# A two-block transformer on one core: two expert pairs written out ahead of TensorE's loop, transposed rows copied out one PSUM bank at a time, and the last gathers held back

## The reference, cut to what matters

```
g_w        = softmax(h @ grp_w + b)[g_sel]
e_p, e_i   = top_k(softmax(expert logits of that group), 2)
weight     = g_w * e_p / sum(e_p)
hid        = silu(xb @ w_gate[e]) * (xb @ w_up[e])
out[tok]  += (hid @ w_down[e]) * weight
```

## Time and profile before

| | us |
|---|---|
| median of 3 runs | 2176.9 (2175.75 to 2178.42) |
| the profiled execution | 2185.39 |
| its span in the trace | 2183.7 |
| PE busy | 1885.3 (86% of the span) |
| DVE busy | 1046.7 (48%) |
| ACT busy | 558.5 (26%) |

### The profile page before, as it was taken

One profiled execution on the slowest core, in us unless ns is written; L12 is line 12 of the kernel. 1 busy time (PEld: TensorE's weight loads), 2 busy tenths in 40 slices (PEclk: granted clock), 3 DMA queues, 4 the chain that ended last, 5 costly groups with the idle time before them and its releaser, 6 DMA issues.

```text
span 2183.7 us, 38376 instructions
## 1 busy us (share of the span) xinstructions
PE 1885.3 (86%) x15590; PEld 1368.7 (63%) x15590; DVE 1046.7 (48%) x1922; ACT 558.5 (26%) x1189; POOL 18.8 (1%) x30
## 2 busy tenths in 40 slices
PE   7999987787766789897677777799999999999998
PEld 4744654443433457664344444399988989998997
DVE  5678541010100135542111111377888787788876
ACT  4436631111111123531111110214430021443001
POOL 0100000000000010000000000000000000000000
PEclk9999999999989999998888888999999999999999
DMA  8489249999899994369999999852345545234552
GB/s 360 159 351 426 109 197 402 422 418 429 321 429 429 425 359 179 148 250 423 429 429 428 429 429 429 368 231 105 129 174 193 193 181 235 94 139 174 193 193 97
DMA packets 52501, 628.21 MB, mean 288 GB/s; under 512 B 7088, under 2 KB 8112, under 8 KB 14256
## 3 DMA queue, kind: packets, MB, share of 16 engines
q1 hardware_dynamic: 45008, 611.30, 68.3%
q0 software_dynamic: 2592, 8.91, 1.1%
q10 hardware_dynamic: 4800, 6.56, 0.8%
HBM read 614.43 MB, written 12.32 MB: 287 GB/s over the span
## 4 chain that ended last, share of the span: by engine, by line
PE 52%; DMA 33%; DVE 10%; issue 2%; ACT 1%; SPq 1%; POOL 0%; ACTq 0%; POOLq 0%; DVEq 0%
DMA ring<-in_ex_down 17%; DMA ring<-in_ex_up 14%; PE ps L1435 7%; PE ps L1437 7%; PE ps L1436 6%; PE ps L1917 5%; PE ps L2079 4%; PE ps L2081 4%; PE ps L2080 4%; PE ps L1924 3%; PE ps L1789 1%; DVE w_lo L2987 1%; DMA ring<-in_w_static 1%; PE ps L1817 1%; DVE cat L2507 1%
## 5 line engine op out<-in xcount | busy, mean ns | idle before, releaser
L1917 PE MATMUL ps<-ring,E 128*32 128x256 f32 x5312 | 364.2, 435 | 180.1 <-DMA ring<-in_ex_gate 113.3
L1917 PEld LDWEIGHTS ps<-ring,E 128*32 128x32 f32 x5312 | 214.2, 125 | 337.1 <-issue 270.2
L1437 PE MATMUL ps<-hn_hi,w_lo 128*128 128x256 f32 x928 | 262.3, 283 | 0.0
L1924 PE MATMUL ps<-ring,E 128*32 128x512 f32 x1344 | 163.7, 629 | 31.6 <-DMA ring<-in_ex_down 30.9
L2884 DVE TENSOR_TENSOR E<-E,ps 128x256 f32<-128x256 f32 x25 | 10.5, 422 | 369.0 <-PE ps L1917 369.0
L1437 PEld LDWEIGHTS ps<-hn_hi,w_lo 128*128 128x128 f32 x928 | 177.6, 191 | 0.0
L1435 PE MATMUL ps<-hn_hi,w_lo 128*128 128x256 f32 x480 | 138.2, 288 | 1.7 <-DVE w_lo L2987 1.7
L1436 PE MATMUL ps<-hn_lo,w_lo 128*128 128x256 f32 x480 | 135.6, 283 | 0.0
L2987 DVE TENSOR_TENSOR w_lo<-ring,w_hi 128x4096 fp32r<-128x4096 f32 x30 | 132.8, 4425 | 1.0
L1435 PE MATMUL ps<-hn_hi,w_hi 128*128 128x256 f32 x448 | 126.9, 283 | 0.0
L1436 PE MATMUL ps<-hn_lo,w_hi 128*128 128x256 f32 x448 | 126.8, 283 | 0.0
(11 more groups left out here) (568 smaller groups left out, 3491.2 us busy)
## 6 DMA issues: line engine op xcount, KB each, us to landing
ring<-in_ex_up SPq DMA_DIRECT2D x64, 2048.0 KB, 18.7
ring<-in_ex_gate SPq DMA_DIRECT2D x62, 2048.0 KB, 17.3
ring<-in_ex_down SPq DMA_DIRECT2D x61, 2048.0 KB, 19.2
ring<-in_w_layer SPq DMA_DIRECT2D x56, 2048.0 KB, 8.2
ring<-in_w_static SPq DMA_DIRECT2D x32, 2048.0 KB, 15.3
y_rows<-E ACTq DMA_DIRECT2D x100, 64.0 KB, 7.8
ring<-in_ex_down SPq DMA_DIRECT2D x6, 1024.0 KB, 19.7
y_rows<-pcp POOLq DMA_DIRECT2D x18, 256.0 KB, 10.2
```

Source lines behind the costliest of these rows:

```text
L1437: return pe.matmul(out, lo, xhi, start=False, stop=last)
L1917: ins = pe.matmul(ps[lane(u, h), 2 + w, 0:HALF], xg[:, k, lane(u, h) if j is None else quad(j, u)], weights[u][:, h * HALF:(h + 1) * HALF] ...
L1924: ins = pe.matmul(ps[lane(u, c), bank, :], hid[:, m % 2, lane(u, m // 2)], slab(4 + u, (EC, D))[:, m, half_cols(c)], start=m == 0, stop=m ...
```

## The change

- **A.** The first two pairs of the first mixture stand written out ahead of PE's loop. The plan's wait and PE's two register loads move behind them; the loop runs from 1.
- **B.** `turned_out` copies each bank of transposed rows by itself as soon as its four transposes are done (`xg_mm` counts banks), and `products` waits for the second bank only at k = 4. This holds for both mixtures.
- **C.** In the first mixture the ranks' transpose goes to bank 5 and stands between the two halves of the first `turn`.
- **D.** The first `build` of one-hot matrices no longer steps the slot numbers (`iota2`); that add stands after the `token_low` calls behind it.
- **E.** At the end of the first mixture ACT weights tile 3 behind the root; POOL waits for tile 1's second choice before it issues the four gathers of tiles 2 and 3; SP loads the first w_in slab when tile 1's first choice has landed.

```diff
-            sp.wait_ge(yg_in[1][1], 16)
+            sp.wait_ge(yg_in[1][0], 16)
             static_loads(stream_b)
...
+                act.wait_ge(ssq_mm, ssq_at(call) + KC)
+                act.activation(stdv[...], ps[:, bank, 0:NX], ACT.Sqrt, bias=eps, scale=1.0 / D).then_inc(std_ready, 1)
                 if g == 0:
                     weigh(NTM - 1)
-                act.wait_ge(ssq_mm, ssq_at(call) + KC)
-                act.activation(stdv[...], ps[:, bank, 0:NX], ACT.Sqrt, bias=eps, scale=1.0 / D).then_inc(std_ready, 1)
...
                 def turned_out(count):
-                    act.wait_ge(sems["xg_mm"], count)
-                    at = turn_bank(l)
-                    act.activation(xg, ps[:, at:at + 2, :]..., ACT.Copy).then_inc(sems["xg_ready"], 1)
+                    for c in range(2):
+                        act.wait_ge(sems["xg_mm"], 2 * count - 1 + c)
+                        act.activation(xg[:, 4 * c:4 * c + 4, :], ps[:, turn_bank(l) + c, :]..., ACT.Copy).then_inc(sems["xg_ready"], 1)
...
                 gather(1, True)
                 if l == 0:
+                    turn(1, (0,))
                     pe.wait_ge(m_ready, 2)
-                    pe.matmul(ps[0:1, 2, 0:MAXB], rsc[:, 7, 0:1], ident[:, 0:MAXB], start=True, stop=True).then_inc(pos_mm, 1)
+                    pe.matmul(ps[0:1, 5, 0:MAXB], rsc[:, 7, 0:1], ident[:, 0:MAXB], start=True, stop=True).then_inc(pos_mm, 1)
+                    turn(1, (1,))
+                    pe.sem_inc(sems["gu_mm"], 2)
...
-                    pe.wait_ge(plan_ready, 1)
-                    pairs = pe.value_load(...)
-                    final = pe.value_load(...)
-                    pe.sem_inc(sems["gu_mm"], 2)
...
                         for k in range(KC):
+                            if j == 0 and w == 0 and k % 4 == 0:
+                                pe.wait_ge(sems["xg_ready"], 2 * s + 3 + k // 4)
...
-                with pe.Fori(0, final) as s:
+                for j in range(2):
+                    pair(0, j, False)
+                pe.wait_ge(plan_ready, 1)
+                pairs = pe.value_load(...)
+                final = pe.value_load(...)
+                with pe.Fori(1, final) as s:
                     pair(s, 0, False)
                     pair(s, 1, False)
...
-                    dve.tensor_tensor(iota2, iota2, lane_step, ALU.add)
+                    if not first:
+                        dve.tensor_tensor(iota2, iota2, lane_step, ALU.add)
...
             for n in range(NTM):
+                if n == QT:
+                    pool.wait_ge(yg_in[1][1], 16)
                 for k in range(2):
                     pool.indirect_dma_start(out=yg[n][k], ...).then_inc(yg_in[n][k], 16)
```

More of the change, by code:

```diff
@@ L916, in group_stats @@
                     act.activation(sqb[:, k % 4, 0:NX], xT[:, g, k, :], ACT.Square).then_inc(sq_ready, 1)
+                act.wait_ge(ssq_mm, ssq_at(call) + KC)
+                act.activation(stdv[:, g * NX:g * NX + NX], ps[:, bank, 0:NX], ACT.Sqrt, bias=eps, scale=1.0 / D).then_inc(std_ready, 1)
                 if g == 0:
                     weigh(NTM - 1)
-                act.wait_ge(ssq_mm, ssq_at(call) + KC)
-                act.activation(stdv[:, g * NX:g * NX + NX], ps[:, bank, 0:NX], ACT.Sqrt, bias=eps, scale=1.0 / D).then_inc(std_ready, 1)
             def group_modulate(call, g):
@@ L1147, in turned_out @@
                 def turned_out(count):
-                    act.wait_ge(sems["xg_mm"], count)
-                    at = turn_bank(l)
-                    act.activation(xg, ps[:, at:at + 2, :].rearrange("p b (k s) -> p (b k) s", s=PAIR), ACT.Copy).then_inc(sems["xg_ready"], 1)
+                    for c in range(2):
+                        act.wait_ge(sems["xg_mm"], 2 * count - 1 + c)
+                        act.activation(xg[:, 4 * c:4 * c + 4, :], ps[:, turn_bank(l) + c, :].rearrange("p (k s) -> p k s", s=PAIR), ACT.Copy).then_inc(
+                            sems["xg_ready"], 1)
                 def gathered(count, first=False):
@@ L1155, in gathered @@
                     turned_out(count)
+                act.sem_inc(sems["xg_ready"], 2)
                 gathered(1, True)
@@ L1903, in experts @@
                     keep_x(0)
-                turn(1)
-                if l == 1:
+                    turn(1)
                     pe.wait_ge(mod_ready, 2 + 1)
                     keep_x(1).then_inc(sems["gu_mm"], 2)
-                else:
-                    pe.wait_ge(plan_ready, 1)
-                    pairs = pe.value_load(blki[0:1, MAXB:MAXB + 1], min_val=NE // 2, max_val=MAXB // 2)
-                    final = pe.value_load(blki[0:1, FINAL:FINAL + 1], min_val=NE // 4 - 1, max_val=MAXB // 4 - 1)
-                    pe.sem_inc(sems["gu_mm"], 2)
                 pe.sem_inc(sems["y_mm"], 1)
@@ L1947, in pair1 @@
                         for k in range(KC):
+                            if w == 0 and k % 4 == 0:
+                                pe.wait_ge(sems["xg_ready"], 2 * i + 3 + k // 4)
                             ins = inner(w, k, [SPARE[u][k] if spare and w == 0 else slab(2 * w + u, (KC, DE))[:, k, :] for u in range(2)])
@@ L1998, in experts, with products @@
                     return
-                def products(i, j, beside):
+                def products(s, j, beside):
                     for w in range(2):
                         for u in range(2):
-                            pe.wait_ge(sems["w_in"][2 * w + u], 16 * i + 16)
+                            pe.wait_ge(sems["w_in"][2 * w + u], 16 * (2 * s + j) + 16)
                         for k in range(KC):
+                            if j == 0 and w == 0 and k % 4 == 0:
+                                pe.wait_ge(sems["xg_ready"], 2 * s + 3 + k // 4)
                             ins = inner(w, k, [slab(2 * w + u, (KC, DE))[:, k, :] for u in range(2)], j)
@@ L2013, in pair @@
                     i = 2 * s + j
-                    if j == 0:
-                        pe.wait_ge(sems["xg_ready"], s + 1)
-                    products(i, j, lambda: None)
+                    products(s, j, lambda: None)
                     if not last:
@@ L2029, in pair @@
                     ins.then_inc(sems["y_mm"], 1)
-                with pe.Fori(0, final) as s:
+                for j in range(2):
+                    pair(0, j, False)
+                pe.wait_ge(plan_ready, 1)
+                pairs = pe.value_load(blki[0:1, MAXB:MAXB + 1], min_val=NE // 2, max_val=MAXB // 2)
+                final = pe.value_load(blki[0:1, FINAL:FINAL + 1], min_val=NE // 4 - 1, max_val=MAXB // 4 - 1)
+                with pe.Fori(1, final) as s:
                     pair(s, 0, False)
@@ L2043, in last_rows @@
                     ins.then_inc(selt_mm, 1)
-                products(2 * final + 1, 1, last_rows)
+                products(final, 1, last_rows)
                 pe.wait_ge(sems["hid_ready"], pairs)
@@ L2778, in share_of, with build @@
                     link(dve.tensor_reduce(halves[:, 0:1], below[:, 0:n], AX_X, ALU.add))
-                def build(count):
+                def build(count, first=False):
                     for n in range(nt):
@@ L2820, in experts @@
                     link(dve.tensor_tensor(slotf[:, 0:nt, :], slotf[:, 0:nt, :], later, ALU.add))
-                    build(0)
+                    build(0, True)
                     for q in range(3, 8):
                         token_low(q)
+                    dve.tensor_tensor(iota2, iota2, lane_step, ALU.add)
                     past = rsc[:, 10, 0:1]
@@ L2832, in experts @@
                     dve.wait_ge(pos_mm, 2)
[L2833 removed]
+                    link(dve.tensor_scalar(blkf[0:1, 0:MAXB], ps[0:1, 5, 0:MAXB], float(NE - 1), None, ALU.min))
                     dve.tensor_scalar(fresh[:, 0:1], blkf[0:1, 0:1], 0.0, None, ALU.not_equal)
```

2 lines of the change are left out of this document (removed).

## The result

The changed kernel took 2183.87 us (median of 9 runs, 2182.9 to 2189.08), the kernel before, run beside it, 2178.42 us (9 runs, 2175.75 to 2186.32). The ratio is 1.0022 [1.0011, 1.0032], some 4.8 us slower [2.4, 7.0]. A second set of runs gave 1.0018 [1.0006, 1.0030]. Forecast were 2176.3 us, within 2171.5 to 2181.0: the measured time lies above that, on the side that had a chance of 0.12. The profiled execution took 2185.09 us, its span is 2183.4 us.

The account below looks back on a forecast made before the run. The prediction took the first mixture as limited by weight loads that PE's first products release, and later stretches by PE. Start -4.2 plus end +3.6 gave -0.6 us, from 2176.9 to 2176.3 us, range 2171.5 to 2181.0.

Parts of the forecast that it names:

- -4.2 forecast: Start of the first mixture: loads 3.95 us earlier, plus 0.24 us of wait saved in the second mixture.
- Rivals 3 and 4: At the start: 3, low clock stays, +0.9 us, chance 0.13; 4, SP paces the loads, not PE, +3.4 us, chance 0.07.
- +2.3 us: End of first mixture: tile 2's held gather takes 6.0 us, so the root ends at 816.72 instead of 814.41.
- +1.3: End of first mixture: PE's stand lowers its clock in the sums of squares, costing 1.3 us, within 0 to 3.7.
- Rival 2: End of first mixture: the held gather waits out the slab; +4.5 us in all, 2181.4 us, chance 0.12.
- Rival 1: End of first mixture: held gathers land at once, in 4.2 us, clock stays; -4.5 us in all, 2172.4 us, chance 0.18.

Follow-up runs that it names:

- start alone: The changed kernel with the three edits of E undone, so parts A to D only: 2175.86 us, ratio 0.9979 [0.9970, 0.9987] against the kernel before.
- end alone: The kernel before with only part E made: 2190.42 us, ratio 1.0047 [1.0033, 1.0060] against the kernel before.
- once more: The kernel before, with no edit, run again against itself: 2183.25 us, ratio 1.0012 [1.0001, 1.0022].
- the one without the hold: The changed kernel without POOL's wait, root first and early slab kept: 2175.03 us, ratio 0.9972 [0.9960, 0.9985] against the kernel before.
- register loads alone: The kernel before with part A and the ranks' row in bank 5, whole turn and one copy kept: 2177.25 us, ratio 0.9988 [0.9972, 1.0004].

## Why the prediction was wrong, point by point

**The start was right.** First products 2.5 us earlier (2.47 forecast), full clock (1.7 us, 1.5 forecast), up load 4.2 us earlier (3.95). That the stream of loads follows PE's first products is borne out: the first gather comes 4.6 us earlier behind `sel` in the changed kernel and 5.6 in the start alone, and the latter is 4.6 us faster by the runs (-4.2 forecast). Rivals 3 and 4 fall. The third pair waits 1.48 us for gate's weights instead of 1.40, and DMA still ends that wait, so the moved register loads are covered, as taken; in the second mixture the wait of 0.24 us is gone. Two slips of the sum did no harm: the four k ahead of ACT's second half last half of 3.66, some 1.8 us, not 0.9, and 319.44 - 315.45 is 3.99, not 3.95.

**The end failed, by its size.** The step was "+2.3 us" for the held gather, "+1.3" for the clock, sum +3.6. The mechanism was named rightly: `weigh(2)` ahead of the squares, PE's stand, low clock. The trace has the root 8.1 us later than the kernels with the old end (25.7 against the 17.5 to 17.8 of three of four traces); with the start's -4.2 this makes +3.9, where the two sets of runs have +4.8 and +3.9. From the forecast's 3.6 to 8.1 are four steps:

- The base, +2.5 us. The sum set the new end against a root that had waited 2.43 us for tile 3, and credited that wait as a gain of the new order. The other three traces of the old order don't have it. One profile was read as if it were the kernel; the 11.1 us of the earlier trace rows could have warned, being tile 3's (its first choice, which made the wait, took 11.0, its second 11.1). That first choice was also not issued while the slab came in, as the prediction has it, but 2.2 us ahead of the slab.
- The landing, +1.9 us. 6.0 us were taken between 4.2 and 11.1; tile 2's gather took 7.9 (7.4 to 7.9 in the five traces with hold and early slab). The prediction gave the slab 5 us, so that the gather would meet its second half. The slab took 8.4 us from issue to landing, and the gather was issued 1.5 us behind it, not 2.85.
- The clock, +1.1 us. The sums took 2.45 us more, not 1.3. The 1.5 us at the start came from a low stretch that covered some 3 of 8.84 us; here the clock is 0.50 from 806.82 to 811 us, 4.2 of 6.14 us.
- The release, -1.0 us. POOL issued 9.5 us behind its first gather; 10.6 had been worked out. Tile 1's second choice landed 0.4 us earlier behind the first gather than before, and 0.26 us passed from there to the issue, not 0.84.

These give 3.6 + 2.5 + 1.9 + 1.1 - 1.0 = 8.1.

The Trainium skill ("DMA: Bandwidth & Descriptors", section "Anatomy of one DMA — SWDGE (gpsimd) path") gives, as an estimate, 3.2 us for a gather of 512 KB. No trace here agrees: the first gather took 4.2 to 4.4, a held one without the slab 5.3, beside the slab 7.4 to 7.9. By the Trainium skill (the same page, section "Queues, rings and completion order") each DMA engine takes turns between the queues that have work. The 2.1 to 2.6 us that moving the slab away took off fit that, but would fit a gather that waits out the slab as well.

**The rival on this side had the right place.** Rival 2 said that the held gather waits out the slab, and in all five traces with hold and early slab tile 2's first choice landed 1.0 to 1.1 us behind the slab (805.20 and 804.24 in the changed kernel). It was to decide from a landing of 6.6 us; it landed at 7.9 and the time was 2183.9, above the 2181.4 that this rival gave with 11.1 us, since the base was wrong there too. Its chance of 0.12 was too small: the 6.0 us were the median of eight gathers of which four had landed before the slab went out (the fourth at 804.01, the slab at 804.03), while the held one was issued behind it on purpose. Rival 1 falls with the same 7.9 us.

**What stays open.** From `sel` to the first product with the slab the traces make 518.7 us of the changed kernel (the same in its second trace), 517.7 and 517.4 of before, 524.1 of the end alone and 509.6 of the start alone. So by the traces of before the change costs 1.0 to 1.3 us, the end alone 6.4 to 6.7, and the start alone gains about 8; the runs say 3.9 to 4.8, 10.2 [7.2, 13.0] and 4.6. All three differ by some 3 us in the same direction. As much lies between two sets of runs of the kernel before on one chip: 2180.0 us in the set that the ratios use, and 2183.25 in "once more", whose traced execution (2182.42) is the fifth fastest of its twelve. Against that second set the start alone gains 7.4 us and the end alone costs 7.2, near the traces. So the traces of before seem to show it as the slower set had it. Where the faster runs gain their 3 us was not shown; the root (20.1 in the one trace) and the slab (1.68 us of waiting in the other), both late against the start alone, are candidates. The sizes of the two halves are uncertain by that much; the 10 us between the changed kernel and the one without the hold don't use the kernel before. Open, too, is why removing PE's stand gave back more in the runs than the 2.1 us of its trace; the stretch from the first product with the slab to the second mixture's first varied between traces from 139.5 to 144.4 us.

## What to carry to other kernels

Before a transfer is held back, look up where its consumer stands in the list of the engine that waits for it: held data cost nothing that the runs could tell behind the root and 8 to 10 us in front of it, with the same issue and landing times. A stall that a change is to remove should be seen in more than one execution; here the one profile showed 2.43 us that three others of the same order did not have. And what stands behind a stall pays twice if PE stands with it: 6.46 us of idle PE made 3.69 us of sums into 6.14.

## What the runs showed of the hardware that was not expected

- The POOL instruction that issues a gather took 0.93 to 1.00 us, but in each trace one of the eight took longer: the first behind POOL's wait (1.93 us), or, where nothing is held, the seventh (1.28 to 1.98 us). In the kernel before:

```profile
801.85 1.93 POOL L3255 DMA_INDIRECT E<-y_rows,sloti  x1 [0.31 <-issue]
```

- What PE did before its clock fell, or did not fall: idle 2.03 us ahead of the first products, they took 8.84 us, with a granted clock of 0.50 in 313 to 314 us; idle 1.11 us (register loads alone), 7.11 us at 1.00. Idle 4.11 us ahead of the sums, they took 5.28 us; idle 6.46, 6.14; with idle products in the gap, 3.72 at 1.00. The length of one stand does not decide it alone: 8 us ahead of those first products PE had stood 2.07 us (299.85 to 301.92), and the clock stayed at 1.00.
- The first gather of tile 3, in the same order of lists, landed after 7.1 us in one execution of the kernel before and after 11.0 in the other.
